# Two token blocks in one chain: a triangular solve in 64-column arrays and 64 x 64 tiles, with the recurrence in alternation and the state-space products in quarter tiles

## What is computed

```python
decay = jnp.where(incl, jnp.exp(jnp.where(incl, diff, 0.0)), 0.0)
m = jnp.where(strict, jnp.einsum("bhnid,bhnjd->bhnij", kb, k) * decay, 0.0)
a_mat = m + jnp.eye(CHUNK, dtype=m.dtype)
sol = lax.linalg.triangular_solve(a_mat, rhs, left_side=True, lower=True, unit_diagonal=True)
qk = jnp.where(incl, jnp.einsum("bhnid,bhnjd->bhnij", q, k) * decay, 0.0)
def step(s, inp):
    v_new = uc - jnp.einsum("bhck,bhkv->bhcv", wc, s)
    o = jnp.einsum("bhck,bhkv->bhcv", qd, s) + jnp.einsum("bhij,bhjv->bhiv", qkc, v_new)
    s = s * gl[..., None, None] + jnp.einsum("bhck,bhcv->bhkv", kd, v_new)
```

```python
bu = jnp.einsum('bsgh,gph->bsgp', uf.astype(jnp.complex64), b_bar)
_, states = lax.associative_scan(combine, (a_el, bu), axis=1)
y = jnp.einsum('bsgp,ghp->bsgh', states, c_mat).real + d.astype(f32) * uf
```

## Time and profile before

| | us |
|---|---|
| median of three runs | 2645.27 |
| lowest and highest | 2644.47, 2646.27 |
| the profiled execution | 2644.37 |
| its span, first to last instruction | 2642.6 |
| TensorE busy in the span | 2550.9 (97%) |
| VectorE busy | 1649.5 (62%) |
| ScalarE busy | 1059.2 (40%) |
| GpSimd busy | 368.2 (14%) |

### The profile page before, as it was taken

The page is one execution under the profiler, slowest core; times in us unless marked ns, Lnnn a source line. Parts: engine busy times, 40 slices in busy tenths (PEclk is TensorE's granted clock), DMA queues, the critical chain, the costliest instruction groups (busy, mean ns, idle before and its releaser), DMA issues.

```text
span 2642.6 us, 29766 instructions
## 1 busy us (share of the span) xinstructions
PE 2550.9 (97%) x12186; PEld 2115.6 (80%) x12186; DVE 1649.5 (62%) x1640; ACT 1059.2 (40%) x895; POOL 368.2 (14%) x372
## 2 busy tenths in 40 slices
PE   7989999899999999999999999999999999999998
PEld 6768887688778788888888888888888788888776
DVE  5385566854667755445544557689999964445564
ACT  4543325433234353443344344443332445544332
POOL 0002310131000000000000000027878500000000
PEclk9999999999999999999999999999999999999999
DMA  6332225332465445555555555666555566566553
GB/s 244 124 115 101 102 101 176 111 104 88 140 240 215 185 175 191 191 190 190 187 186 188 191 187 200 217 240 210 180 187 182 188 253 243 176 244 233 199 223 143
DMA packets 84645, 478.63 MB, mean 181 GB/s; under 512 B 8752, under 2 KB 8880, under 8 KB 32944
## 3 DMA queue, kind: packets, MB, share of 16 engines
q1 hardware_dynamic: 84528, 476.99, 50.2%
HBM read 453.88 MB, written 23.07 MB: 180 GB/s over the span
## 4 chain that ended last, share of the span: by engine, by line
PE 74%; DVE 16%; DMA 4%; issue 4%; ACT 2%; SPq 0%; DVEq 0%; ACTq 0%
PE acc L1974 21%; PE acc L1976 21%; PE acc L1975 21%; DVE w_lo L1237 4%; PE banks L2154 4%; DMA raw<-in_w 3%; PE banks L2177 2%; DVE prod L1754 2%; ACT w_hi L792 2%; PE banks L1985 1%; DVE squares L1453 1%; DVE convT L1443 1%; DVE prod L1748 1%; PE banks L2085 1%; DVE prod L1747 1%
## 5 line engine op out<-in xcount | busy, mean ns | idle before, releaser
L1237 DVE TENSOR_TENSOR w_lo<-raw,w_hi 128x2048 fp32r<-128x2048 f32 x396 | 915.1, 2314 | 643.6 <-ACT w_hi L792 642.6
L792 ACT ACTIVATE w_hi<-raw 128x2048 fp32r<-128x2048 f32 x396 | 755.2, 1913 | 632.7 <-DMA raw<-in_w 632.5
L1974 PE MATMUL acc<-w_hi,a_hi 128*128 128x512 f32 x2112 | 850.5, 403 | 32.4 <-DVE w_lo L1237 24.5
L1976 PE MATMUL acc<-w_hi,a_lo 128*128 128x512 f32 x2112 | 827.5, 392 | 0.0
L1975 PE MATMUL acc<-w_lo,a_hi 128*128 128x512 f32 x2112 | 827.0, 392 | 0.0
L1974 PEld LDWEIGHTS acc<-w_hi,a_hi 128*128 128x128 f32 x2112 | 400.0, 189 | 128.0 <-DVE w_lo L1237 22.2
L1976 PEld LDWEIGHTS acc<-w_hi,a_lo 128*128 128x128 f32 x2112 | 398.9, 189 | 85.9
L1975 PEld LDWEIGHTS acc<-w_lo,a_hi 128*128 128x128 f32 x2112 | 400.0, 189 | 81.0 <-issue 1.9
L1974 PE MATMUL acc<-w_hi,b_hi 128*128 128x512 f32 x928 | 365.1, 393 | 0.0
L1976 PE MATMUL acc<-w_hi,b_lo 128*128 128x512 f32 x928 | 362.4, 391 | 0.0
L1975 PE MATMUL acc<-w_lo,b_hi 128*128 128x512 f32 x928 | 362.2, 390 | 0.0
(11 more groups left out here) (329 smaller groups left out, 2026.3 us busy)
## 6 DMA issues: line engine op xcount, KB each, us to landing
raw<-in_w SPq DMA_DIRECT2D x396, 1024.0 KB, 4.8
spilled<-stage SPq DMA_DIRECT2D x72, 256.0 KB, 6.0
gate_in<-spilled SPq DMA_DIRECT2D x20, 512.0 KB, 4.1
b_pad<-in_b_pad SPq DMA_DIRECT2D x8, 512.0 KB, 5.8
x_rows<-in_x SPq DMA_DIRECT2D x4, 512.0 KB, 9.7
x_rows<-in_x SPq DMA_DIRECT2D x1, 2048.0 KB, 12.2
mem_rows<-in_mem SPq DMA_DIRECT2D x2, 1024.0 KB, 4.8
spilled<-stage_b SPq DMA_DIRECT2D x8, 256.0 KB, 6.0
```

The source lines that it names most:

```text
L792: act.activation(w_hi[:, n % HIGH, :], raw[:, n % RAW, :], ACT.Copy)\
L1237: dve.tensor_tensor(w_lo[:, n % RAW, :], raw[:, n % RAW, :], w_hi[:, n % HIGH, :].bitcast(F32), ALU.subtract).then_inc(lo_split, 1)
L1974: pe.matmul(o, hi[:, tk], wh, start=first, stop=False)
L1976: ins = pe.matmul(o, lo[:, tk], wh, start=False, stop=last)
```

## The change

The solve is packed by chunk. In place of 128 x 128 matrices with two chunks on the diagonal, an array now holds 8 matrices of 64 x 64 (two directions, four heads) side by side in 512 columns, chunk 0 of the block in the upper 64 partitions and chunk 1 in the lower. A new function by_chunk makes the products: for each of the eight, one matmul of 64 x 64 x 64 in the upper left tile and one in the lower right tile, into the same bank. Both directions are in one array, and both token blocks go through one chain of steps, so a half has 31 steps in place of 45, over the same places; turn is a matmul with the identity in place of a transpose. The masks are packed alike. In the recurrence both_directions issues the products of the two directions alternately, head by head, and scan_out makes the update of the state ahead of the output. In the state-space stage bu uses 32-row tiles, with one bank for each of a round's two groups, and y 32-column tiles; b is loaded once (1 MB), c_pad and its copies are gone (VectorE writes the spread C matrix c_out once, in ssm_small), VectorE's four products take both groups in one instruction, and a round takes seven half units in place of six. The stage is nine units longer, and the steps behind it come nine units later.

```diff
-    for t in range(NT):
-        s += [("gram", half, t), ("decay", half, t), ("pause",), ("turn", half, t)]
-        for n in range(1, len(LEVELS)):
-            s += [("solve_y", half, t, n), ("solve_x", half, t, n)]
+    s += [("gram", half), ("decay", half), ("pause",), ("turn", half)]
+    for n in range(1, len(LEVELS)):
+        s += [("solve_y", half, n), ("solve_x", half, n)]
...
-SSM_STRIDE = 3
+SSM_PLACES = 7
...
-    for ct in range(KW):
-        put(a + 2 * SSM_STRIDE * ct, "load_b_pad", ct)
+    put(a, "load_b")
     put(a, "ssm_u")
     for i in range(17):
         for part, place in enumerate((0, 2, 3, 5)):
-            put_at(2 * (a + 3 + SSM_STRIDE * i) + 1 + place, "ssm", i, part)
-    a += 3 + SSM_STRIDE * 17
+            put_at(2 * (a + 3) + 1 + SSM_PLACES * i + place, "ssm", i, part)
+    a += 3 + -(-SSM_PLACES * 17 // 2)
...
-                if i % 2 == 0:
...
-                            for a_ in range(4):
-                                col = 160 * a_ + 16 * u
-                                pool.tensor_copy(c_pad[rs, kk, z, col:col + 16], c_eff[rs, z, 4 * ct + a_, :])\
-                                    .then_inc(pool_done, me.done(f"cpad{ct}"))
...
+                for t in range(NT):
+                    w = per_chunk(t)
...
+                    dve.tensor_tensor(both(w[MAT]), many(b[:, 0:256], 2), both(w[INV]), ALU.mult)\
+                        .then_inc(dve_done, me.done(f"decay{half}{t}.M"))
+                    dve.tensor_tensor(both(w[ATT]), many(b[:, 256:512], 2), both(w[EXP]), ALU.mult)\
+                        .then_inc(dve_done, me.done(f"decay{half}{t}.Q"))
...
+            def turn(half):
                 dve.wait_ge(dve_done, me.here())
...
+                    dve.tensor_tensor(pairs(w[INV]), pairs(w[MAT]), by_head(level[:, 6]), ALU.mult)\
+                        .then_inc(dve_done, me.done())
+                    dve.wait_ge(act_done, me.at(f"turn{half}{t}.MT"))
+                    dve.tensor_tensor(pairs(w[EXP]), pairs(w[MATT]), by_head(level[:, 0]), ALU.mult)\
+                        .then_inc(dve_done, me.done())
+                dve.wait_ge(dve_done, me.here())
+                for t in range(NT):
+                    w = per_chunk(t)
+                    dve.tensor_tensor(eight(w[INV]), many(cols["unit"], 8), eight(w[INV]), ALU.subtract)\
+                        .then_inc(dve_done, me.done(f"turn{half}{t}.X"))
+                    dve.tensor_tensor(eight(w[EXP]), many(cols["unit"], 8), eight(w[EXP]), ALU.subtract)\
+                        .then_inc(dve_done, me.done(f"turn{half}{t}.XT"))
...
+                    dve.wait_ge(pool_done, me.at("c_out.zero"))
+                    for u in range(2):
+                        rs, cs = slice(64 * u, 64 * u + 64), slice(16 * u, 16 * u + 16)
+                        dve.tensor_tensor(c_out[rs, 0, :, cs], c_eff[rs, 0], c_tmp[rs, 0], ALU.subtract)\
+                            .then_inc(dve_done, me.done())
+                        dve.scalar_tensor_tensor(c_out[rs, 1, :, cs], c_eff[rs, 1], -1.0, c_tmp[rs, 1],
+                                                 ALU.mult, ALU.subtract)\
+                            .then_inc(dve_done, me.done("ssm.c_out"))
...
+                    bu = [banks[:, 0:2, z * T:(z + 1) * T] for z in range(2)]
...
+                    dve.wait_ge(pe_done, me.at(f"ssm{i}.bu"))
+                    dve.tensor_tensor(pr[0], bu[0], c_, ALU.mult).then_inc(dve_done, me.done())
+                    dve.tensor_tensor(pr[1], bu[1], s_, ALU.mult).then_inc(dve_done, me.done())
+                    dve.tensor_tensor(pr[2], bu[1], c_, ALU.mult).then_inc(dve_done, me.done())
+                    dve.tensor_tensor(pr[3], bu[0], s_, ALU.mult).then_inc(dve_done, me.done(f"ssm{i}.turned"))
...
+            def by_chunk(b, lhs, rhs, name):
+                for k in range(8):
+                    cs = slice(64 * k, 64 * k + 64)
+                    for c in range(2):
+                        rs = slice(64 * c, 64 * c + 64)
+                        ins = pe.matmul(b[rs, cs], lhs[rs, cs], rhs(k, rs), start=True, stop=True)
+                ins.then_inc(pe_done, me.done(name))
...
+            def turn(half):
+                for z, x, to in (("M", MAT, "MT"), ("Q", ATT, "QT")):
+                    for t in range(NT):
+                        pe.wait_ge(dve_done, me.at(f"decay{half}{t}.{z}"))
+                        b = take_bank(f"turn{z}{half}{t}", 0, f"turn{half}{t}.{to}")
+                        by_chunk(b, per_chunk(t)[x], lambda k, rs: ident[rs, rs], f"turn{half}{t}.{z}")
+            def solve_y(half, n):
+                for t in range(NT):
+                    w = per_chunk(t)
+                    before = f"turn{half}{t}.X" if n == 1 else f"solve{half}{t}{n - 1}.X"
+                    pe.wait_ge(dve_done, me.at(before))
+                    pe.wait_ge(pool_done, me.at(f"solve{half}{t}{n}.Mt"))
+                    b = take_bank(f"solveY{half}{t}{n}", 0, f"solve{half}{t}{n}.Yc")
+                    by_chunk(b, w[SUM], lambda k, rs: w[INV][rs, 64 * k:64 * k + 64], f"solve{half}{t}{n}.Y")
+            def solve_x(half, n):
+                for t in range(NT):
+                    w = per_chunk(t)
+                    pe.wait_ge(act_done, me.at(f"solve{half}{t}{n}.Yc"))
+                    pe.wait_ge(dve_done, me.at(f"turn{half}{t}.XT" if n == 1 else f"solve{half}{t}{n - 1}.XT"))
+                    b = take_bank(f"solveT{half}{t}{n}", 0, f"solve{half}{t}{n}.XT")
+                    last = n == len(LEVELS) - 1
+                    by_chunk(b, w[MAT], lambda k, rs: w[EXP][rs, 64 * k:64 * k + 64],
+                             f"solve{half}{t}{n}.Z" if last else f"solve{half}{t}{n}.ZT")
+                    if not last:
+                        b = take_bank(f"solveZ{half}{t}{n}", 0, f"solve{half}{t}{n}.X")
+                        by_chunk(b, w[EXP], lambda k, rs: w[MAT][rs, 64 * k:64 * k + 64], f"solve{half}{t}{n}.Z")
...
+            def both_directions(pairs):
                 for hd in range(4):
+                    for b, rs, lhs, rhs, names in pairs:
+                        ins = pe.matmul(b[rs, hd * P:(hd + 1) * P], lhs(hd), rhs(hd), start=True, stop=True)
+                        if hd == 3:
+                            ins.then_inc(pe_done, me.done(*names))
...
+                pe.wait_ge(dve_done, me.at(f"scan{half}.{st - 1}.S0", f"scan{half}.{st - 1}.S1"))
+                for tag, x, z in (("scanP", kT, "P"), ("scanO", qT, "O")):
+                    pairs = []
+                    for d in range(2):
+                        c, t, rs = chunk_of(st, d)
+                        b = take_bank(f"{tag}{half}{st}", d, f"scan{half}.{st}.r{d}")
+                        lhs = lambda hd, x=x, tk=slice(64 * c, 64 * c + 64): x[:, hd, tk]
+                        rhs = lambda hd, d=d: state[:, d, hd, :]
+                        names = [f"scan{half}.{st}.{z}{d}"] + ([f"scan{half}.{st}.in.PE"] if z == "O" and d else [])
+                        pairs.append((b, rs, lhs, rhs, names))
+                    both_directions(pairs)
...
                     b = take_bank(f"scanN{half}{st}", d, f"scan{half}.{st}.vnew{d}")
+                    lhs = lambda hd, d=d, t=t, rs=rs: solT[rs, t, 4 * d + hd, :]
+                    if st:
+                        rhs = lambda hd, d=d, rs=rs: RG(d)[rs, hd * P:(hd + 1) * P]
+                    else:
+                        rhs = lambda hd, t=t, rs=rs: v_rows[rs, t, hd, :]
+                    pairs.append((b, rs, lhs, rhs, [f"scan{half}.{st}.new{d}"]))
+                both_directions(pairs)
...
+                    v = lambda hd, d=d, rs=rs: EB(d)[rs, hd * P:(hd + 1) * P]
                     if st < 3:
                         b = take_bank(f"scanS{half}{st}", d, f"scan{half}.{st}.S{d}")
+                        lhs = lambda hd, d=d, t=t, rs=rs: k_dec[rs, d, t, hd, :]
+                        decayed.append((b, slice(0, P), lhs, v, [f"scan{half}.{st}.dS{d}"]))
+                both_directions(decayed)
+                for d in range(2):
+                    c, t, rs = chunk_of(st, d)
+                    v = lambda hd, d=d, rs=rs: EB(d)[rs, hd * P:(hd + 1) * P]
+                    b = take_bank(f"scanQ{half}{st}", d, f"scan{half}.{st}.out.DVE")
+                    lhs = lambda hd, d=d, t=t, rs=rs: qkT[rs, t, 4 * d + hd, :]
+                    within.append((b, rs, lhs, v, [f"scan{half}.{st}.o2{d}"]))
+                both_directions(within)
...
+                    b = [this_bank(g, f"bu{i}", g, f"ssm{i}.turned") for g in range(2)]
+                    for z in range(2):
+                        for g in range(2):
+                            rs = slice(64 * (i % 2) + 32 * g, 64 * (i % 2) + 32 * g + 32)
+                            ins = pe.matmul(b[g][:, z * T:(z + 1) * T], b_in[rs, ct, z, :], uT[rs, ct, :],
                                             start=True, stop=True)
+                    ins.then_inc(pe_done, me.done(f"ssm{i}.bu"))
```

(7 more changed lines are left out.)

362 lines of the change are left out of this document (133 added, 229 removed).

## The result

The changed kernel takes 2544.04 us (median of four runs, 2543.45 to 2544.75) where the one before takes 2645.23 beside it: a ratio of 0.9614, with a 95% interval of 0.9602 to 0.9625. The forecast was 2526, with 2508 to 2548 for its own case. The time is in the range. The gain was 100 us of span where 119 were expected: the terms for the matmuls came out, the one for TensorE's standing did not, and what is worth learning is which terms of the sum were exact and which were not.

What follows compares the result with a forecast made beforehand. TensorE, busy 97% of the span, was taken to bound the kernel through its matmuls and standing. Gains of 46.8, 24.6, 28 and 19.5 sum to 118.9 us, giving 2526 us; range 2508 to 2600, own case 2508 to 2548.

Steps and rivals of the forecast that it cites:

- products of the solve: Delta halves: 64 x 64 products in paired tiles cost 37.5 us a half for 60.9, gaining 46.8 us in both.
- recurrence's products: Delta rule's recurrence: alternating the directions makes its matmul part 20.0 us a half for 32.3, gaining 24.6 in both.
- standing in the delta halves and the conv ahead: TensorE's waits and slow clock in the delta halves: 28 of 38 us gained (15 to 30); conv ahead nothing, ±3.
- state-space stage: Paired row and column tiles cut its excess over streaming from 63.1 to 43.6 us, gaining 19.5.
- The number on which the case rested: Price of a solve pass with two 64-column tiles paired: 0.028 us, with 0.056 as upper bound without overlap.
- Rival B: Solve: paired tiles in one bank take turns, or loads share one path; 0.056 us a pass, 2590 us; chance 0.16.
- rival C: Solve: each change of tile costs as a change of shape does; 2752 us, slower; chance 0.07.
- rival D: Only the state-space tiles do not pair; 2552 us; chance 0.07.
- rival E: Solve: TensorE's gains turn into waits for VectorE, so the delta stage gives them back; near no change; chance 0.02.
- Unit 23 and 55 still bound them on VectorE: nothing, ±3.: Conv steps ahead of the solve: they keep their place to within half a slot, gaining nothing, ±3 us.
- 1.3 to 1.4 with the way between engines: Recurrence: scan_new's wait in us for both directions' right sides, at five of six places, 7 us in all.
- Each keeps its distance to the next: Steps behind the state-space stage: all move nine slots with distances kept; no loss was counted.

Runs made afterwards that it cites:

- run with the conv parts apart: On top of right sides first in scan_in and later steps one unit earlier: one empty place between the conv's two parts in each half; 2509.41 us, ratio 0.9482.
- run with both edits: Changed kernel with scan_in's right sides made before anything for the queries, and steps behind the state-space stage one unit earlier; 2523.03 us, ratio 0.9537.
- additions last: Changed kernel with scan_in's additions into the output rows moved behind both directions' right sides; 2535.9 us, ratio 0.959.
- right sides first: Changed kernel with both key products and right sides made before anything for the queries in scan_in, whose banks their own products release; 2532.18 us, ratio 0.9572.

## Why the forecast was right, and where not

The terms, in us of span (the parts found are the excesses of the stages, less what the pass prices give for the matmuls):

| term | forecast | found | from |
|---|---|---|---|
| products of the solve | 46.8 | 45.6 | 1152 x 0.029 + 13 x 0.36 = 38.1 for 60.9 in a half |
| recurrence's products | 24.6 | 24.2 | 20.2 for 32.3 in a half |
| standing in the delta halves and the conv ahead | 28 | 15.8 | below |
| state-space stage | 19.5 | 22.4 | 63.1 − 40.7 |
| steps behind it | 0 | −10.7 | the excess from there to unit 360, 31.2 before and 41.9 after |
| everything else | 0 | 3.0 | the remainder to 100.3 |

**The matmuls.** The number on which the case rested came out: 0.029 for 0.028. It prices the whole solve, and not only the steps that it was read from: where nothing stands, in the last stretch shown, the solve of half 0 costs 39.9 us above its streaming, for 38.1 by the prices and some 0.9 for eight transposes of the conv that lie in it. It was read off two tiles that met by chance in the kernel before and halved for half the columns. Rival B is refuted by the group of 0.98 us, and rival C with it; rival D by the state-space stage, and rival E by the gain of the solve, which VectorE did not give back. The rule of the Trainium skill, "TensorEngine Tiling (Array Packing)", section Restrictions and Gotchas, by which different row tiles cannot use one PSUM bank at a time, does not hold for these two tiles: they write different partitions of the same bank, 32 passes in 0.98 us, where 64 listed tile by tile take 3.56. These two tiles differ in their columns as well as in their rows; tiles that differ in rows alone had two banks here, so for them no run shows it. The tile-by-tile run shows that the pairing comes from the alternation in the list, less what the engine pairs at a seam.

**The state-space stage.** The price of its groups was right (2.54 us a round for 2.6). The gain is 3 us larger since nothing at all is left of standing. The argument that VectorE decides held: seven half units let TensorE lead, six do not. VectorE's need was overestimated, 20.0 a round (40.03 / 2) for 21.2, and the copies of C are part of the reason: they were called nothing by themselves, which is right on the path to 1.2 us, but with them VectorE's same operations take 41.94.

**Standing.** This step of the sum failed in size, 15.8 for 28, near the lower bound of 15. The delta halves, in which the 28 were looked for, stood 38 us before and 33.7 after (150.3 of excess less 2 x 58.3): they gave 4.3. The conv ahead, which was put at nothing, had 9.9 in each half before and keeps 2.7 and 5.6 (2.7 to 5.9 in other runs whose code is the same there), so 11.5 of the gain lies there, since a stop moved from it into the delta halves. Three things were misjudged.
- "Unit 23 and 55 still bound them on VectorE: nothing, ±3." The bound stayed, but its stop moved. Before, TensorE stood 4.8 us in each half for the conv's result in the conv part; after, it stands 6.9 us for the split of unit 23 and 3.0 in half 1, within the delta halves, with a slow clock behind it. So the 15.6 us of waits for L1498 went as forecast, and 9.9 for splits and 10.3 for the right side stand in the same halves in place of them and of smaller ones. The run with the conv parts apart shows the cause of the splits' part: its two conv stretches (units 20.5 to 26 and 52.5 to 57) are 4.5 and 5.5 us shorter than in the run with both edits.
- "1.3 to 1.4 with the way between engines", for the right side. The sum left out the addition into the output rows (0.69), which stands in VectorE's order between the two right sides. It also left out that VectorE starts on the key products 0.8 us before TensorE is back at the stream (348.72 and 349.50). The two cancel, so that the waits of 1.40 and 1.36 in the last rounds are right by luck. The other three are 2.47, 2.48 and 2.60, with GpSimd's decay of the state beside VectorE's operations, which the sum priced at 0.68 throughout, and in the third a split ahead of them: 10.3 in all for 7.
- "Without the clock falling behind it." In half 0 it fell behind both waits of 2.5 us; in half 1 it did not behind 2.60. The forecast had counted on 1.4, and had itself named stops over 2 us with the clock at 0.50 behind them as a sign of being wrong. The runs with the additions last and with the right sides first take these two errors back in part and whole: by their ratios 6 and 11 us, some 5 either way.

**The steps behind the stage.** "Each keeps its distance to the next" was the wrong step. It looked at the order of the steps and not at SyncE's queue, in which the loads of these steps stand among the stores of the weight groups. Nine units moved two loads from ahead of a store to behind one. The state-space part alone shows the same loss, and one unit earlier takes it back.

Standing and the queue make 22.9 us, the two prices 1.6, and the gains beyond the forecast 5.9; that is the distance of 18.6 from 118.9 to 100.3.

## What to carry to other kernels

A price that decides a case can often be read where two things meet by chance in the trace of the kernel before; there, halving it for half the columns was right to 0.001 us. Alternate the tiles in the list, since the engine paired neighbours here and not runs. When steps are moved, follow each queue that their transfers use, and look at what stands in front of them there; a distance in steps is no distance in a queue. And before a wait is priced, list all operations of the engine that stand ahead of it, also those that nobody waits for, and what GpSimd does beside them.

## What the runs showed of the hardware

- Two tiles of 64 x 64 on the diagonal write one bank at once: 32 passes in 0.98 us; 64 passes with entering and leaving take 2.22 us in alternation and 3.56 listed tile by tile.
- A change into small tiles and back among streaming matmuls costs 0.36 us with 64 x 64 tiles and 0.39 with the state-space stage's row and column tiles (2.54 us a round, for two groups of four pairs of 0.22).
- Some of VectorE's operations get longer while GpSimd works. Two of scan_in that read no bank take 0.95 and 1.53 us beside GpSimd's decay of the state and 0.69 each without it; one beside it that reads a bank (308.00) takes 0.69. In the state-space stage the same 41 operations take 40.03 us with 24.88 of GpSimd beside them and 41.94 with 36.23.
- After a stop of 2.47 us TensorE's granted clock was 0.62 over the next 4.5 us, a mix of its two levels (1.2 and 2.4 GHz); in the run with the right sides first, with waits of at most 0.5 there, no such stretch stands in the recurrence of half 0. Behind a stop of 2.60 us in half 1 it stayed at 1.00, so the length of a stop alone does not say whether the clock falls.
